# Band attention by pairs of heads in one pipeline over all tiles, its inputs made inside the last recurrence turns

## The chip, the cores and the metric

One core of one Trainium2 chip runs the whole program. The time is device microseconds of one execution; the kernel before has a median of 4641.96 us over 3 runs (4640.98 to 4644.14). Its engines are TensorE (PE, with its weight loads as PEld), VectorE (DVE), ScalarE (ACT), GpSimd (POOL) and SyncE (SP, which only issues transfers here).

## The reference

One layer of a streaming encoder, for a prompt of 2048 frames and a sample group of 32 frames. A combined projection feeds an RWKV-7 recurrence and a band attention; both are gated, merged and followed by an MLP. The change touches the attention (8 heads of 64):

```python
def band_attend(q, k, v, bias, valid):
    s = jnp.einsum("bqhd,bkhd->bhqk", q, k).astype(jnp.float32) * ATT_SCALE + bias
    s = jnp.where(valid, s, jnp.finfo(jnp.float32).min)
    p = jax.nn.softmax(s, axis=-1).astype(v.dtype)
    return jnp.einsum("bhqk,bkhd->bqhd", p, v)
```

In the prompt each chunk of 64 frames attends to its own chunk and the 8 before it. In the sample group 32 new frames attend to 256 cached frames and themselves. The bias comes from a table of relative distances, one row for each head.

## The kernel before

The program is a row of stages: modulation and first norm; the projection's first 14 row tiles; the recurrence in 34 turns of 64 frames (`build_rwkv`, line 1045), in which turns 1 to 28 also carry the projection's remaining 28 row tiles; the two final states (`store_states`, line 1178); the attention; the merge; the MLP. Stages are blocks, and a block begins when all engines have ended the one before. Inside a block each engine runs its own list in the order in which the code was written, and semaphores (`Steps`, line 65) tie the lists together.

A recurrence turn (`tensor_turn`, line 925) is a chain of small 64x64 products, each of which waits for VectorE or ScalarE to take the last result. `fill(n)` between the links issues up to n products of the projection. In turns 29 to 34 nothing is left to fill with, so `fill` does nothing there. On SP a turn loads the next rows (`sync_chunk`, line 674) and stores the output of the turn before it (`store_chunk`, line 679), which waits for VectorE's last step of that output.

The attention is `build_attention` (line 1211). `build_attention_inputs` (line 1227) loads q, k and v of all frames, turns v from channels to frames with TensorE transposes (L1285, copied out at L1303), turns the last 512 frames of k for an output (L1292), and makes the bias of each head by reversing rows of the table of distances (L1307). Then `build_attention_core` (line 1487) runs over 16 tiles of 128 queries, with up to 640 keys each: tiles 0 to 3 have 128, 256, 384 and 512 keys, tiles 4 to 15 have 640. For a tile VectorE copies the window of k and of v (L1522, L1529) and ScalarE the scaled queries (L1423).

Within a tile (class `Heads`, line 1340) the heads go one by one. TensorE makes the scores of a head from 64 rows of the array (L1460). VectorE adds the bias and takes the maximum (L1390). ScalarE takes the exponentials and their sum (L1433). VectorE makes the reciprocal (L1396) and scales the probabilities (L1399). TensorE turns them in five blocks (L1471), VectorE copies two blocks out (L1418) and ScalarE three (L1439). TensorE multiplies them with v (L1482): its stationary operand is the 128 columns of v of two heads, of which 64 output rows are used. The order on each engine is written out in `Heads.__init__`; head h's transposes are followed by the scores of head h+2 and by head h's values. At a tile's end ScalarE copies the result out (L1444) and stores it. A further block does the 32 sample queries against 288 keys in the same way, after loading and turning the cache (L1563 to L1584).

## Time and profile before

| what | us |
|---|---|
| median of 3 runs | 4641.96 |
| the profiled execution | 4652.85, of which the span is 4651.1 |
| start to the end of the projection's first part | 533.0 |
| recurrence turns 1 to 28 | 1312 |
| recurrence turns 29 to 34 and the states | 197.3 |
| attention (inputs, 16 tiles, sample tile) | 589.3 |
| merge and MLP | 2019.5 |

TensorE is busy for 91% of the span, DVE for 38%, ACT for 29%, POOL for 11%. [...]

### The profile page before, as it was taken

Reading aid. Unit: us, or ns where it says so; the run is one execution under the profiler, and the core shown is the slowest. Engines: PE = TensorE matmul, PEld = TensorE weight load, DVE = VectorE, ACT = ScalarE, POOL = GpSimd, SP = SyncE. Lnnn points to the kernel's source line nnn. Section 1 sums busy time; section 2 is a strip of 40 time slices with the busy share of each in tenths; the row PEclk is TensorE's granted clock in tenths of the full one; section 3 lists DMA queues with packets and bytes.
Section 4 is the critical chain, followed back from the end, with each engine's and each line's share of the span. In section 5 each row is a group of like instructions: output and inputs, shape, how many; then the busy total and the mean of one; then the engine's idle time right before and its main releaser. Section 6 shows DMA issues by size and latency. Waiting matters only on the chain. (4 is left out here: it accounts for less than half of the span.)

```text
span 4651.1 us, 83037 instructions
## 1 busy us (share of the span) xinstructions
PE 4222.8 (91%) x34634; PEld 3823.3 (82%) x34634; DVE 1763.5 (38%) x3403; ACT 1329.0 (29%) x2378; POOL 532.3 (11%) x518
## 2 busy tenths in 40 slices
PE   6799799999999999748888699979999999999998
PEld 2499688888888888746666489969999999999997
DVE  3500033333333333434555443335354453453542
ACT  2311122222222222103344321234343343443432
POOL 2211122332323232300000000000000000000000
PEclk9899899999999999665899699989999999999999
DMA  6522221212121211040000333334334344343342
GB/s 220 169 70 70 52 53 43 54 43 54 43 54 43 56 43 44 15 141 27 9 9 7 95 117 121 98 104 130 110 109 138 114 120 125 108 143 109 109 128 78
DMA packets 595783, 392.82 MB, mean 84 GB/s; under 512 B 99312, under 2 KB 585352, under 8 KB 594448
## 3 DMA queue, kind: packets, MB, share of 16 engines
q1 hardware_dynamic: 528336, 309.63, 23.6%
q10 hardware_dynamic: 67136, 78.63, 4.9%
q8 instruction: 246, 4.03, 0.4%
q14 instruction: 65, 0.53, 0.0%
HBM read 306.87 MB, written 81.34 MB: 83 GB/s over the span
## 5 line engine op out<-in xcount | busy, mean ns | idle before, releaser
L527 PE MATMUL proj_ps<-h_hi,w_hi 128*128 128x416 f32 x1680 | 619.8, 369 | 13.4 <-POOL w_lo L512 13.4
L527 PE MATMUL proj_ps<-h_lo,w_hi 128*128 128x416 f32 x1680 | 600.2, 357 | 0.0
L527 PE MATMUL proj_ps<-h_hi,w_lo 128*128 128x416 f32 x1680 | 596.2, 355 | 0.0
L1999 DVE TENSOR_TENSOR ff_lo<-ff_raw,ff_hi 128x1024 fp32r<-128x1024 f32 x320 | 391.5, 1224 | 450.1 <-ACT ff_hi L1995 449.8
L1600 PE MATMUL ff_ps<-h_hi,ff_hi 128*128 128x416 f32 x1280 | 462.8, 362 | 25.0 <-DVE ff_lo L1999 23.9
L1995 ACT ACTIVATE ff_hi<-ff_raw 128x1024 fp32r<-128x1024 f32 x320 | 337.7, 1056 | 454.4 <-PE ff_ps L1600 432.7
L1600 PE MATMUL ff_ps<-hidden_hi,ff_hi 128*128 128x416 f32 x1280 | 459.5, 359 | 3.8 <-DVE ff_lo L1999 3.8
L1600 PE MATMUL ff_ps<-h_hi,ff_lo 128*128 128x416 f32 x1280 | 452.4, 353 | 0.0
L1600 PE MATMUL ff_ps<-hidden_hi,ff_lo 128*128 128x416 f32 x1280 | 451.7, 353 | 0.0
L1600 PE MATMUL ff_ps<-h_lo,ff_hi 128*128 128x416 f32 x1280 | 448.3, 350 | 0.0
L1600 PE MATMUL ff_ps<-hidden_lo,ff_hi 128*128 128x416 f32 x1280 | 447.3, 349 | 0.0
L527 PEld LDWEIGHTS proj_ps<-h_hi,w_hi 128*128 128x128 f32 x1680 | 316.1, 188 | 32.2 <-issue 13.6
L527 PEld LDWEIGHTS proj_ps<-h_hi,w_lo 128*128 128x128 f32 x1680 | 316.4, 188 | 8.0
L527 PEld LDWEIGHTS proj_ps<-h_lo,w_hi 128*128 128x128 f32 x1680 | 317.6, 189 | 5.0
L935 PEld LDWEIGHTS wkv_ps<-solve 64*64 64x64 f32 x6336 | 213.7, 140 | 74.7 <-issue 53.8
L1600 PEld LDWEIGHTS ff_ps<-h_hi,ff_hi 128*128 128x128 f32 x1280 | 241.0, 188 | 36.4 <-DVE ff_lo L1999 21.7
L935 PE MATMUL wkv_ps<-solve 64*64 64x64 f32 x6336 | 245.8, 228 | 15.3 <-ACT solve L845 15.2
L1600 PEld LDWEIGHTS ff_ps<-hidden_hi,ff_hi 128*128 128x128 f32 x1280 | 240.3, 188 | 11.8 <-DVE ff_lo L1999 5.2
L1600 PEld LDWEIGHTS ff_ps<-h_lo,ff_hi 128*128 128x128 f32 x1280 | 241.5, 189 | 8.7 <-issue 5.1
L1600 PEld LDWEIGHTS ff_ps<-hidden_lo,ff_hi 128*128 128x128 f32 x1280 | 240.6, 188 | 8.8 <-issue 5.1
L1600 PEld LDWEIGHTS ff_ps<-h_hi,ff_lo 128*128 128x128 f32 x1280 | 240.6, 188 | 1.9
L1600 PEld LDWEIGHTS ff_ps<-hidden_hi,ff_lo 128*128 128x128 f32 x1280 | 240.0, 188 | 1.7
(285 smaller groups left out, 6587.8 us busy)
## 6 DMA issues: line engine op xcount, KB each, us to landing
ff_raw<-in_w_ff SPq DMA_DIRECT2D x320, 512.0 KB, 4.1
keep_proj<-proj_out ACTq DMA_DIRECT2D x210, 208.0 KB, 1.9
ada_w<-in_w_ada SPq DMA_DIRECT2D x24, 1024.0 KB, 5.7
w_raw<-in_w_in SPq DMA_DIRECT2D x42, 512.0 KB, 4.7
gates<-keep_proj SPq DMA_DIRECT2D x80, 208.0 KB, 2.5
rows_in<-keep_proj SPq DMA_DIRECT2D x32, 448.0 KB, 6.0
x_then_x<-keep_xT SPq DMA_DIRECT2D x40, 208.0 KB, 2.5
keep_x2T<-x_then_x ACTq DMA_DIRECT2D x40, 208.0 KB, 1.9
```

The lines of the kernel that those rows point to most:

```text
L527: mm = pe.matmul(self.ps[u][:, 0:BW], w[:, par, kk, :], a[:, kk, cols], start=(kk == 0 and j == 0), stop=(kk == KD - 1 and j == 2))
L935: mm = pe.matmul(self.bank[bank][rows, at + j * C:at + (j + 1) * C], lhs[rows, j, :], rhs[rows, j, :], start=True, stop=True)
L1600: mm = pe.matmul(out, w(i), x(kt), start=(first and i == 0 and j == 0), stop=(last and i == n - 1 and j == 2))
L1995: w.hi_s.done(act.activation(w.whi[:, s % 2], w.raw[:, s % 4], ACT.Copy), s)
L1999: w.lo_s.done(dve.tensor_tensor(w.wlo[:, s % 2], w.raw[:, s % 4], w.whi[:, s % 2].bitcast(F32), ALU.subtract), s)
```

## The change

Two things are changed.

First, the attention's inputs are made inside turns 29 to 33 by a new class `AttentionInputs`. The first recurrence block's setup also makes the table of distances, scaled by 8. q, k, v and the bias lie where the projection's inputs were, which are dead by then. In each of these turns there are five slots. In a slot TensorE makes four transposes of 128x128 in the place of the old filling work, and ScalarE copies the result out in the place where it used to take a projection result. There are 24 slots: 17 for v, 2 for the cache's k, 5 for the k output. VectorE reverses two heads' bias at the end of each of four turns. SP loads what the slots need between its own loads and stores.

Second, the core works on a pair of heads at once, and one software pipeline of 68 pairs plus two closing rounds runs over all 16 prompt tiles and the sample tile, with no block boundary and no loop between them. In round i TensorE makes the scores of pair i, the transposes of the first head of pair i-1, the values of pair i-2, and the transposes of the second head of pair i-1. Scores of the two heads use rows 0 to 63 and 64 to 127 of the array, by turns; values of the two heads use columns 0 to 63 and 64 to 127, by turns. q, k and v are read where they lie, so the three copies for a tile are gone. The probabilities are no longer scaled: the sums of a tile's 8 heads are inverted by one instruction, spread over 64 rows each by 8 products (L1512 after), copied by ScalarE, and multiplied into the result by VectorE, once for a tile.

The diff, cut to its core (the classes `Heads` and the functions `build_attention_inputs` and `build_attention_core` of before are removed, and `build_attention` is empty):

```diff
@@ build_rwkv
+    prep = AttentionInputs(outer, nc, k, pj, FILLED + RT + 1)
...
+                    if t > FILLED:
+                        prep.sync_turn(sp, t - FILLED - 1)
...
                             pj.evacuate(act, t + RT + 1, 1 - par, b)
+                        else:
+                            prep.scalar_slot(act, SLOTS * (t - FILLED - 1) + b)
...
+                    if t > FILLED:
+                        prep.vector_turn(dve, t - FILLED - 1)
...
-                    products = pj.products(pe, t + RT + 1, 1 - par) if filled(t) else iter(())
+                    products = pj.products(pe, t + RT + 1, 1 - par) if filled(t) else prep.products(pe, t - FILLED - 1)
...
+    build_attention_core(nc, k, prep)
...
+class AttentionInputs:
...
+    def sync_turn(self, sp, i):
+        if i == 0:
+            self.pj.mm_s.wait(sp, NB - 1, self.last)
+            self.pj.wait_stored(sp, IN_T)
+        for n in range(SLOTS * i, min(SLOTS * i + SLOTS, self.staged)):
+            kind, j = self.slots[n]
+            if n >= STAGES:
+                sp.wait_ge(self.turned, n - STAGES + 1)
...
+            sp.dma_start(out, src).then_inc(self.loaded[n % STAGES], 16)
+        if i < NH // 2:
+            for h in (2 * i, 2 * i + 1):
+                if h >= 2:
+                    sp.wait_ge(self.bias_turned, h - 1)
...
+            sp.dma_start(self.kT, self.rows[:, KT_:KT_ + NP, :]).then_inc(self.qk_loaded, 16)
+            sp.dma_start(self.qT, self.rows[:, QT:QT + NP, :]).then_inc(self.qk_loaded, 16)
...
+    def products(self, pe, i):
+        for n in range(SLOTS * i, SLOTS * i + SLOTS):
+            for place in range(3 * KD):
+                if place == KD and n < len(self.slots):
+                    self.tensor_slot(pe, n)
+                yield
...
+            mm = pe.transpose(ps[0:src.shape[1], a * P:(a + 1) * P], src, self.k.ident[:, :])
+        mm.then_inc(self.turned, 1)
...
+            act.activation(self.V[0:rows_of_tile(j), j, :], ps[0:rows_of_tile(j), :], ACT.Copy).then_inc(self.kept, 1)
...
+                dve.tensor_copy(self.bias[:, h, :], self.rev[:, h % 2, ::-1]).then_inc(self.bias_turned, 1)
...
+def build_attention_core(nc, k, a):
...
+                def scores(i):
+                    b, j = pair(i)
+                    if i >= 1:
+                        biased.wait(pe, 1, i - 1)
+                    halves = [b.keys(rows, j) for rows in HALVES]
+                    for n in range(len(halves[0])):
+                        for h, rows in enumerate(HALVES):
+                            x0, x1, keys = halves[h][n]
+                            mm = pe.matmul(ps_s[h][0:b.nq, x0:x1], a.qT[rows, j, b.cols], keys, start=True, stop=True)
+                    made_scores.done(mm, "s")
+
+                def turned(i, h):
+                    b, j = pair(i)
+                    exped.wait(pe, h, i)
+                    if i + h >= 1:
+                        front_kept.wait(pe, 1 - h, i - 1 + h)
+                        back_kept.wait(pe, 1 - h, i - 1 + h)
+                    for c, n in b.chunks:
+                        part = c // (2 * P) if c < 2 * P else 1
+                        at = c - 2 * P * part
+                        mm = pe.transpose(ps_t[0:n, part, at:at + b.nq], e[0:b.nq, i % 2, h, c:c + n], k.ident[0:b.nq, 0:b.nq])
+                    made_turned.done(mm, h)
+
+                def values(i):
+                    b, j = pair(i)
+                    front_kept.wait(pe, 1, i)
+                    back_kept.wait(pe, 1, i)
+                    if j == 0 and b.t >= 1:
+                        normed.wait(pe, "y", b.t - 1)
+                    if j == 0 and b.sample:
+                        pe.wait_ge(sample_loaded, 32)
+                    for n, (c, size) in enumerate(b.chunks):
+                        for h, rows in enumerate(HALVES):
+                            mm = pe.matmul(ps_y[rows, j, 0:b.nq], b.values(c, size, slice((2 * j + h) * HD, (2 * j + h + 1) * HD)),
+                                           eT[0:size, i % 2, h, c:c + b.nq], start=(n == 0), stop=(n == len(b.chunks) - 1))
+                    made_values.done(mm, "y")
+                    if j == NP - 1:
+                        divided.wait(pe, "r", b.t)
+                        for jj in range(NP):
+                            for h, rows in enumerate(HALVES):
+                                mm = pe.matmul(ps_r[rows, jj, 0:b.nq], rec[0:b.nq, b.t % 2, 2 * jj + h:2 * jj + h + 1].broadcast_to([b.nq, HD]),
+                                               k.ident[0:b.nq, 0:b.nq], start=True, stop=True)
+                        spread.done(mm, "r")
+
+                for i in range(N + 2):
+                    if i < N:
+                        scores(i)
+                    if 1 <= i <= N:
+                        turned(i - 1, 0)
+                    if i >= 2:
+                        values(i - 2)
+                    if 1 <= i <= N:
+                        turned(i - 1, 1)
...
+                def add_bias(i, h):
+                    b, j = pair(i)
+                    made_scores.wait(dve, "s", i)
+                    if i >= 2:
+                        made_turned.wait(dve, h, i - 2)
+                    dve.memset(idle[:, 0, 2 * (i % 2) + h:2 * (i % 2) + h + 1], 0.0)
+                    biased.done(dve.tensor_tensor_reduce(e[0:b.nq, i % 2, h, b.c0:b.c1], ps_s[h][0:b.nq, b.c0:b.c1], bias(b, 2 * j + h),
+                                                         -(HD ** -0.5), 3.0e38, ALU.add, ALU.min,
+                                                         nmax[0:b.nq, b.t % 2, 2 * j + h:2 * j + h + 1]), h)
+
+                def keep_front(i, h):
+                    b, j = pair(i)
+                    made_turned.wait(dve, h, i)
+                    if i >= 2:
+                        made_values.wait(dve, "y", i - 2)
+                    ins = take_turned(dve.tensor_copy, b, i % 2, h, 0)
+                    front_kept.done(dve.memset(idle[:, 1, 2 * (i % 2) + h:2 * (i % 2) + h + 1], 0.0) if ins is None else ins, h)
+
+                def divide(t):
+                    exped.wait(dve, 1, t * NP + NP - 1)
+                    nq = bands[t].nq
+                    divided.done(dve.reciprocal(rec[0:nq, t % 2, :], total[0:nq, t % 2, :]), "r")
+
+                def norm(t):
+                    spread_kept.wait(dve, "r", t)
+                    if t >= 2:
+                        dve.wait_ge(stored[t % 2], 16 * (t // 2))
+                    nq = bands[t].nq
+                    normed.done(dve.tensor_tensor(yT[:, t % 2, :, 0:nq], ps_y[:, :, 0:nq], rb[:, :, 0:nq], ALU.mult), "y")
+
+                for i in range(N + 2):
+                    if i < N:
+                        add_bias(i, 0)
+                    if 1 <= i <= N:
+                        keep_front(i - 1, 0)
+                    if i < N:
+                        add_bias(i, 1)
+                    if 1 <= i <= N:
+                        keep_front(i - 1, 1)
+                        if i % NP == 0:
+                            divide(i // NP - 1)
+                    if i >= 2 and (i - 2) % NP == NP - 1:
+                        norm((i - 2) // NP)
...
+                def exponentials(i, h):
+                    b, j = pair(i)
+                    biased.wait(act, h, i)
+                    s = e[0:b.nq, i % 2, h, b.c0:b.c1]
+                    at = 2 * j + h
+                    exped.done(act.activation(s, s, ACT.Exp, bias=nmax[0:b.nq, b.t % 2, at:at + 1], scale=-1.0,
+                                              accum_out=total[0:b.nq, b.t % 2, at:at + 1]), h)
...
+                def keep_spread(t):
+                    spread.wait(act, "r", t)
+                    if t >= 1:
+                        normed.wait(act, "y", t - 1)
+                    nq = bands[t].nq
+                    spread_kept.done(act.activation(rb[:, :, 0:nq], ps_r[:, :, 0:nq], ACT.Copy), "r")
+
+                for i in range(N + 2):
+                    if 1 <= i <= N:
+                        keep_back(i - 1, 0)
+                    if i < N:
+                        exponentials(i, 0)
+                        exponentials(i, 1)
+                    if 1 <= i <= N:
+                        keep_back(i - 1, 1)
+                    if i >= 2 and (i - 2) % NP == NP - 1:
+                        keep_spread((i - 2) // NP)
```

The order of TensorE inside a full tile. The names are the scores' banks, the turned probabilities' bank and the output's bank; "x5" means five such instructions in a row. Before, one head in the loop over tiles, transposes of head h, scores of head h+2, values of head h:

```order
L1471 MATMUL probs_ps<-identity,probs 128x128 x5
L84 REGISTER_ALU
L1460 MATMUL scores_ps<-k_window,q_tile 128x512
L1460 MATMUL scores_ps<-k_window,q_tile 128x128
L84 REGISTER_ALU
L84 ISA
L84 REGISTER_ALU x2
L1482 MATMUL att_ps<-probs_turned,v_window 128x128 x5
```

After, the last round of a tile, with its closing products:

```order
L1480 MATMUL scores_ps<-kT,qT 128x512 x2
L1480 MATMUL scores_ps<-kT,qT 128x128 x2
L1492 MATMUL probs_ps<-identity,scores 128x128 x5
L1505 MATMUL proj_ps<-probs_turned,v_rows 64x128 x10
L1512 MATMUL proj_ps<-identity,prob_recips 64x128 x8
L1492 MATMUL probs_ps<-identity,scores 128x128 x5
```

One head's group was 5 transposes, 2 scores and 5 values. Now a round holds 4 scores, 5 transposes, 10 values and 5 transposes for two heads, and one round in four also the 8 products that spread the reciprocals. The rows L84, which move registers and waits for the loop over tiles, are gone.

The order of SP from turn 28 to turn 30, with the semaphores that each transfer waits for. `keep_yrT` is the store of a turn's output, `rows_in` the load of a later turn's rows. Before:

```order
L681 DMA keep_yrT<-yr_out 128x4x64 [waits state_dve]
L676 DMA rows_in<-keep_proj 128x14x64 [waits front_pool]
L681 DMA keep_yrT<-yr_out 128x4x64 [waits state_dve]
L676 DMA rows_in<-keep_proj 128x14x64 [waits front_pool]
L681 DMA keep_yrT<-yr_out 128x4x64 [waits state_dve]
```

After:

```order
L682 DMA keep_yrT<-yr_out 128x4x64 [waits state_dve]
L677 DMA rows_in<-keep_proj 128x14x64 [waits front_pool]
L1304 DMA att_rows_in<-keep_proj 128x4x128 [waits proj_stored1,proj_stored0,proj_mm]
L1304 DMA att_rows_in<-keep_proj 128x4x128 x4
L1309 DMA bias_backwards<-keep_ext 128x640 x2
L1312 DMA kT<-keep_proj 128x4x2080
L1313 DMA qT<-keep_proj 128x4x2080
L682 DMA keep_yrT<-yr_out 128x4x64 [waits state_dve]
L677 DMA rows_in<-keep_proj 128x14x64 [waits front_pool]
L1304 DMA att_rows_in<-keep_proj 128x4x128
```

The first loads for the slots wait for the projection's last store. They, the bias rows and the two large loads of k and q now stand between the rows of turn 30 and the output store of turn 28. In turn 30 the slots' loads follow the row load, which follows that store.

## Rows read from the trace of the kernel before

**Rows 1.** Windows: us, busy PE, PEld, DVE, ACT, POOL (instructions), PEclk, DMA, GB/s.
```profile
2042.30:2107.60 65.30, 20.81 (x92) 14.81 (x92) 18.24 (x32) 3.60 (x6) 0.00 (x0) 0.55 0.82 275
2107.60:2208.00 100.40, 86.62 (x350) 66.26 (x352) 43.15 (x199) 38.40 (x107) 0.00 (x0) 0.59 0.03 9
2146.70:2179.40 32.70, 29.18 (x106) 23.32 (x106) 11.56 (x51) 11.22 (x28) 0.00 (x0) 0.50 0.03 9
2208.00:2590.70 382.70, 327.05 (x1824) 248.31 (x1822) 211.97 (x599) 152.50 (x324) 0.00 (x0) 0.89 0.03 8
2590.70:2631.60 40.90, 24.54 (x96) 16.19 (x96) 10.80 (x52) 8.41 (x29) 0.00 (x0) 0.54 0.12 34
```

**Rows 2.** Timeline, one head of a full tile: start us, us, engine, line, operation.
```profile
2351.09 1.34 PE L1460 MATMUL scores_ps<-k_window,q_tile 64*128 64x512 f32 x4
...
2352.36 1.38 PE L1482 MATMUL att_ps<-probs_turned,v_window 128*128 128x128 f32 x10
2352.47 0.82 DVE L1390 CUSTOM_DVE_ANT_0 scores<-scores_ps,bias 128x640 f32<-128x640 f32 x1 [0.20 <-issue]
...
2353.34 0.83 ACT L1433 ACTIVATE probs<-scores,minus_max 128x640 f32<-128x640 f32 x1 [1.65 <-DVE minus_max L1390]
...
2353.58 0.71 PE L1471 MATMUL probs_ps<-identity,probs 128*128 128x128 f32 x5
...
2354.22 1.34 PE L1460 MATMUL scores_ps<-k_window,q_tile 64*128 64x512 f32 x4
2354.32 0.49 ACT L1439 ACTIVATE probs_turned<-probs_ps 128x384 f32<-128x384 f32 x1
2354.32 0.42 DVE L1418 COPY probs_turned<-probs_ps 128x256 f32<-128x256 f32 x1 [1.02 <-PE probs_ps L1471]
```

**Rows 3.** Waits of PE in the twelve full tiles: total us, times, longest.
```profile
PE probs_ps L1471 <- ACT probs L1433: 34.8, 11, 3.2
```

**Rows 4.** Timeline of TensorE in a late turn, products over 64 rows.
```profile
1992.97 0.42 PE L956 MATMUL wkv_ps<-lora_w_in,w_a_up 64*128 64x64 f32 x1
...
1993.18 0.42 PE L956 MATMUL wkv_ps<-lora_w_in,w_a_up 64*128 64x64 f32 x1
1993.19 0.42 PE L957 MATMUL wkv_ps<-rows_mixed,w_a_up 64*128 64x64 f32 x1
```

**Rows 5.** Windows of 10 us where the granted clock rises.
```profile
2180.00:2190.00 10.00, 7.51 (x29) 5.38 (x26) 4.34 (x16) 3.55 (x9) 0.00 (x0) 0.50 0.08 26
2190.00:2200.00 10.00, 10.00 (x60) 7.75 (x61) 6.16 (x24) 3.90 (x10) 0.00 (x0) 0.96 0.01 2
```

**Rows 6.** Timeline and DMA issues: the attention's inputs.
```profile
2047.54 1.97 PE L1285 MATMUL v_ps<-identity,vT 128*128 128x128 f32 x8 [0.17 <-DMA vT<-keep_proj]
...
qT<-keep_proj SPq DMA_DIRECT2D x1, 4160.0 KB, 29.4
```

**Rows 7.** Late turns: first and last start, last projection store, output store, row loads.
```profile
L956 PE MATMUL wkv_ps<-lora_w_in,w_a_up x32: 417/418/473, 1881.9 to 1994.0; 64*128 64x64 f32 x32
...
1846.33 0.34 ACTq L541 DMA_DIRECT2D keep_proj<-proj_out  x1
...
1988.55 0.38 SPq L681 DMA_DIRECT2D keep_yrT<-yr_out  x1
...
rows_in<-keep_proj SPq DMA_DIRECT2D x3, 448.0 KB, 4.3
```

**Rows 8.** Softmax passes of tiles 0 to 3, min/median/max ns.
```profile
L1433 ACT ACTIVATE probs<-scores,minus_max x32: 385/554/723, 2108.0 to 2202.6; 128x128 f32<-128x128 f32 x8, 128x256 f32<-128x256 f32 x8, 128x384 f32<-128x384 f32 x8, 128x512 f32<-128x512 f32 x8
```

**Rows 9.** Timeline of the sample tile: loads, scores, last store.
```profile
2595.44 0.46 SPq L1564 DMA_DIRECT2D v_window<-in_cache_att_v  x1
2600.07 1.57 PEld L1572 LDWEIGHTS scores_ps<-identity,cache_k_rows 128*128 128x128 f32 x8 [9.62 <-DMA v_window<-in_cache_att_v]
...
2603.56 1.17 PE L1460 MATMUL scores_ps<-k_window,q_tile 64*32 64x288 f32 x4 [1.51 <-DVE k_window L1581]
...
2629.42 0.39 ACTq L1446 DMA_DIRECT2D keep_yaT<-att_turned  x1
```

More of the change, by code:

```diff
@@ new lines, with __init__, keys, values @@
+class Band:
+    def __init__(self, a, t):
+        self.t, self.sample = t, t == NQ
+        self.nq = DEC if self.sample else P
+        self.c0, self.c1 = (0, SKEYS) if self.sample else (max(KT5 - 1 - t, 0) * P, BAND)
+        self.cols = slice(t * P, t * P + self.nq)
+        self.chunks = [(c, min(P, self.c1 - c)) for c in range(self.c0, self.c1, P)]
+        self.a = a
+    def keys(self, rows, j):
+        a = self.a
+        if self.sample:
+            return [(0, PAST, a.Kc[rows, j, :]), (PAST, SKEYS, a.kT[rows, j, SEQ:NT])]
+        at = (self.t - KT5 + 1) * P
+        return [(x0, x1, a.kT[rows, j, at + x0:at + x1]) for x0, x1 in ((self.c0, 512), (512, BAND)) if x1 > x0]
+    def values(self, c, n, cols):
+        a = self.a
+        if self.sample:
+            return a.Vc[:, c // P, cols] if c < PAST else a.V[0:n, NQ, cols]
+        return a.V[0:n, self.t - KT5 + 1 + c // P, cols]
@@ new lines, in build_attention_core @@
+        spread = Steps(ctx, nc, "att_recips_spread", ["r"])
+        biased = Steps(ctx, nc, "att_biased", [0, 1])
+        exped = Steps(ctx, nc, "att_exped", [0, 1])
+        front_kept, back_kept = Steps(ctx, nc, "att_turned_front_kept", [0, 1]), Steps(ctx, nc, "att_turned_back_kept", [0, 1])
+        divided = Steps(ctx, nc, "att_sums_divided", ["r"])
+        spread_kept = Steps(ctx, nc, "att_recips_kept", ["r"])
+        normed = Steps(ctx, nc, "att_normed", ["y"])
+        bands = [Band(a, t) for t in range(TILES)]
@@ new lines, in pair, with bias, take_turned @@
+        def pair(i):
+            return bands[i // NP], i % NP
+        def bias(b, h):
+            return sbias[:, h, :] if b.sample else a.bias[:, h, b.c0:b.c1]
+        def take_turned(copy, b, par, h, part):
+            first, full, last = b.c0 // P, b.c1 // P, (b.c1 + P - 1) // P
+            ins = None
+            for n, t0, t1 in ((P, first, full), (b.c1 - full * P, full, last)):
+                t0, t1 = max(t0, 2 * part), min(t1, (2, KT5)[part])
+                if t1 > t0:
+                    out = eT[0:n, par, h, t0 * P:t1 * P].rearrange("p (c t) -> p c t", t=P)[:, :, 0:b.nq]
+                    ins = copy(out, ps_t[0:n, part, (t0 - 2 * part) * P:(t1 - 2 * part) * P].rearrange("p (c t) -> p c t", t=P)[:, :, 0:b.nq])
+            return ins
@@ L1278, in _ @@
+                sp.dma_start(a.Vc, k.cache_v.rearrange("(c p) h d -> p c (h d)", p=P)).then_inc(sample_loaded, 16)
+                out = k.yaT.rearrange("(a p) t -> p a t", p=P)
+                for t, b in enumerate(bands):
+                    normed.wait(sp, "y", t)
+                    sp.dma_start(out[:, :, b.cols], yT[:, t % 2, :, 0:b.nq]).then_inc(stored[t % 2], 16)
+                for j in range(2):
+                    sp.wait_ge(stored[j], 16 * ((TILES + 1 - j) // 2))
             @block.tensor
@@ L1300, in _ @@
-                dve.tensor_copy(ext[:, near:EXT], tab[:, 2 * REL:2 * REL + 1].broadcast_to([NH, EXT - near])).then_inc(made, 1)
-                for j in range(NQ + 1):
-                    dve.wait_ge(turned, j + 1)
-                    dve.tensor_copy(a.V[0:size(j), j, :], pv[j % 2][0:size(j), :]).then_inc(kept, 1)
-                    if j % 2 == 1:
-                        h = j // 2
-                        dve.wait_ge(back[h % 4], 16 * (h // 4 + 1))
-                        dve.tensor_copy(a.bias[:, h, :], rev[:, h % 4, ::-1]).then_inc(bias_turned, 1)
@@ L1595, in split_products, with build_attention @@
+def build_attention(nc, k):
+    pass
 def split_products(pe, out, hi, lo, x_hi, x_lo, kts, first=True, last=True):
```

457 lines of the change are left out of this document (147 added, 310 removed).

## The prediction

> **What bounds the kernel now.** I read the page's row of the granted clock first, then windows cut at the stages, then the timeline inside one tile, then the waits of TensorE. The windows [rows 1] split the stage that changes: 65.3 us until the first bias is added, in which TensorE is busy for 20.8; 100.4 us for tiles 0 to 3 at a mean granted clock of 0.59; 382.7 us for the twelve full tiles at 0.89, 31.9 us each; 40.9 us for the sample tile.
>
> Inside a full tile at full clock TensorE is the bound [rows 2]: the scores of a head start at 2351.09, its neighbour's values at 2352.36, the next transposes at 2353.58, the next scores at 2354.22. So scores hold TensorE for 1.27 us, values 1.22, five transposes 0.64, together 3.13 us a head or 25.0 us for eight. [...]
>
> Every stage is a block, so what shortens the attention moves merge and MLP forward unchanged; nothing there is touched. The whole saving shows in the time.
>
> **The start (removed: 65.3 us; added: about 7).** The input block goes. What is left before the first bias is the sample's two loads and one VectorE copy, which waits for both. The same kind of pair takes 4.6 us from the second issue to use in the sample tile [rows 9], plus 0.5 for the first issue; the copy moves the same 32x2304 elements as now, which I put at 1.3 us. That is 6.4 us in place of 65.3: -58.9. The table of distances moves to the recurrence's setup, a chain of two transfers in a block that has a load and a transpose of its own; I take +1 us.
>
> **Turns 29 to 33 (added).** A turn lasts 37 us, a third of 1881.9 to 1992.5 over three turns [rows 7]. Five slots of four transposes come in. [...] Slots 3 to 5 stand where TensorE waits for a copy anyway; the first stands ahead of the link RH, and nothing hides it. ScalarE's copies of 512 columns stand in the chain as the evacuations did. I charge half, 2 us a turn, and 1 us a turn for the first slot's load: it is issued behind the output store (1988.55), the row load and its own issue, lands some 5 us later as row loads do (4.3) [rows 7], and TensorE asks at about 1994.2. That is 15 us for five turns. Once, in turn 29, the wait is longer: the first load waits for the projection's last store, issued at 1846.33 [rows 7]; store (2.3) and load (3) put its landing at about 1852, and TensorE asks at 1846.6. Queued behind that waiting slot is the whole turn: +5. k and q take 29.4 us to land [rows 6], from about 1853 to 1882, just before turn 30's rows and slots are wanted; behind them I see no stall. The eight reversals on VectorE fall between the turn's last VectorE step and the next turn's first product and cost nothing. If that cover went they would cost 4. Sum +20. Bounds: 0 (all hidden, or paid back by a warmer clock) and 45 (24 slots at 0.9 and a copy of 0.6 in the chain, 5 and 5 for loads).
>
> **A full tile (the largest term).** Scores of the two heads lie in rows 0 to 63 and 64 to 127. The trace has such a pair already: L956 and L957 start 0.01 us apart, and the next pair follows after 0.21 us [rows 4]. So two heads' scores should hold TensorE as long as one head's do now, 1.27 us. For values the stationary operand is halved to 64 columns and the two heads sit side by side. No row shows two products that share all 128 rows and differ in columns alone; the nearest are the scores' halves above and the 64x64 quarters of the recurrence, which use both. Bounds: 1.22 us for both heads if they overlap, 2.44 if not; I take 1.22. Transposes stay 0.64 for each head. A pair then holds TensorE for 1.27 + 1.22 + 2 x 0.64 = 3.77 us, against 6.26 now.
>
> Do the waits allow this? I lay one round out from the durations of rows 2: scores to bias 1.39 (their duration and 0.05), bias with its memset and read 0.87, exponentials with the read 0.95, VectorE's copy 0.42, ScalarE's 0.49. With scores at 0: bias of head 0 to 2.26, transposes of the older pair from 1.27 to 1.98, VectorE's copy to 2.70, bias of head 1 to 3.57, next scores possible from 3.62. ScalarE: copy to 2.50, exponentials to 3.45, second exponentials 3.61 to 4.55, copy to 5.04, which is 1.25 into the next round, where TensorE asks for it at 1.27. So both chains close just inside TensorE's 3.77, and the round is 3.8 us. Four rounds are 15.2. A tile's close adds eight pairs of products of 128 columns, 1.0 us, and its ScalarE copy and VectorE multiplication delay the next bias by about half a microsecond, of which 0.4 reaches TensorE: 16.6 us a tile at full clock. The copies of k, v and q (3.0 us of VectorE) and the scaling (0.55 a head) are gone from the path.
>
> [...] Which share of the time is slow? Now it is about 0.2 (0.89 granted). The long seam of 3.2 us is gone, but TensorE no longer has slack against the other engines, and short gaps may come in each round. I take a quarter: 0.75 / 16.6 + 0.25 / 30 tiles a microsecond, 18.7 us a tile, 224 us for twelve against 382.7: -158.7. Bounds: 199 and 360.
>
> **Tiles 0 to 3.** [...] In tile 0 ScalarE is longer, since an exponential pass of 128 keys takes 0.39 us [rows 8] and its read 0.19: 2.3. The clock starts low, as now. It rose in tile 3, when TensorE had no gap for some microseconds (busy 7.51 of 10 us at 0.50, then 10.00 at 0.96) [rows 5]; tile 2, at 29.2 of 32.7 us busy, stayed at 0.50 [rows 1]. I take tiles 0 and 1 slow and 2 and 3 half way to 3.0 and 3.4: 4 x (2.3 + 3.2 + 3.7 + 4.5) + 7 of closes = 62 against 100.4: -38.4. Bounds 51 and 71.
>
> **Sample tile.** No block edge, no cache loading in front. A round is scores 1.17 [rows 9] and two biases with a copy between, 2.6 us; four are 10.4, and the last pair's way out (exponentials, transposes, values, spread, copy, multiplication, store of 2.2 from 2629.42 to the block's end [rows 1, 9]) 6.8. 17.2 against 40.9: -23.7, give or take 5.
>
> **Sum.** -58.9 + 1 + 20 - 158.7 - 38.4 - 23.7 = -258.7. The profiled execution took 4652.85 us (span 4651.1 and 1.75 around it), 10.9 above the median. 4652.85 - 258.7 = 4394; less 10.9, 4383 us beside the median.
>
> **Rivals.**
> [...]
> [...]
> *The values' halves don't overlap.* A round is 1.22 longer at full clock and 2.2 at half: 21.5 and 39 a tile, 24.2 at the same mix; +66 and +10 in the short tiles: 4459 us. Nothing in the trace excludes it.
> *The round is bound by the semaphores, not by TensorE.* The three engines hand over six times a round and my layout closes within 0.1 us. If a round is 4.6 us, TensorE has gaps of 0.8 in each and I put the slow share at 0.4: 0.6 / 19.8 + 0.4 / 30, 22.9 a tile: +50, 4433 us.
> *Slower.* Neither halves overlap, and the low clock holds. Then a round is 4.3 + 4.3 + 2.1 + 0.4 = 11.1 us, a tile 47, against 31.9 now; full tiles +340 and short ones +39 on the forecast: 4762 us. It decides once a full tile takes over 37 us. The rows of L956 and L957 speak against half of it.
>
> **How the numbers follow.** Forecast 0.57, low clock 0.18, values one after the other 0.10, semaphores 0.11, slower 0.03, about no change 0.01. The range reaches down to 4330, where tiles run at full clock (199 and 51) and the turns grow by little, and up to 4530, the low-clock case. A measurement of this kernel can tell 0.2%, about 9 us, from no change. All cases but one lie over 100 us below 4642: faster 0.96, same 0.01, slower 0.03.
>
> **What would show it.** In the profile after: no input block, first bias about 7 us into the attention block; turns 29 to 33 at 39 to 42 us with TensorE waiting about 5 us once for `att_rows_in`; products of the two heads starting within 0.02 us of each other, in L1480 and in L1505; a round of 3.8 us where the clock is 1.00; full tiles at 18.7 us with a granted clock near 0.88; about 17 us for the sample. It is wrong if the clock in the full tiles is near 0.5, if L1505's instructions come one after another, or if turns 29 to 33 grow by more than 45 us.

## The result and the profile after

The changed kernel takes 4326.45 us, median of four runs (4325.18 to 4331.74), against 4643.05 us for the kernel before (4640.98 to 4648.82). The ratio is 0.9315, 95% interval 0.9303 to 0.9326: faster, by 317 us. I had forecast 4383 us with a range from 4330 to 4530. The direction was right, and so was what was to make a tile shorter; the time is 57 us below the forecast and just below the range.

The profiled execution took 4331.74 us (span 4329.7). First the windows of the kernel after, cut as [rows 1] cut the one before (the start, tiles 0 to 3, the full tiles, the sample tile), then three windows of 10 us in tiles 0 and 1. Columns as in [rows 1].

```profile
2043.28:2049.56 6.28, 0.80 (x4) 0.53 (x4) 1.35 (x1) 0.00 (x0) 0.00 (x0) 0.50 0.52 130
2049.56:2095.48 45.92, 43.00 (x365) 29.66 (x366) 20.53 (x133) 30.35 (x97) 0.00 (x0) 0.84 0.06 19
2095.48:2292.48 197.00, 196.94 (x2006) 144.56 (x2006) 120.86 (x408) 132.31 (x300) 0.00 (x0) 1.00 0.06 18
2292.48:2310.64 18.16, 13.20 (x178) 10.61 (x178) 6.83 (x38) 7.43 (x28) 0.00 (x0) 0.79 0.08 20
...
2050.00:2060.00 10.00, 9.41 (x48) 5.69 (x48) 3.38 (x35) 6.01 (x28) 0.00 (x0) 0.50 0.00 0
2060.00:2070.00 10.00, 9.19 (x80) 6.27 (x78) 3.79 (x27) 5.60 (x19) 0.00 (x0) 0.80 0.09 29
2070.00:2080.00 10.00, 9.25 (x99) 6.93 (x99) 5.21 (x32) 7.50 (x21) 0.00 (x0) 1.00 0.10 29
```

The third row is the one to look at: in 197.00 us of full tiles TensorE is busy for 196.94 and the granted clock is 1.00, full speed. Before it was busy for 327.05 of 382.7 at 0.89. The clock is a share of full speed; the records of all these kernels hold 0.50 and 1.00 and nothing else, and a mean between them is a mix of the two. The last three rows show where the full clock begins: the mean of 0.80 in the second of them is 4 us at 0.50 and 6 at 1.00, so it begins some 14 us after the first bias, in tile 1. The kernel before was at 0.50 until tile 3 [rows 5], 83 us after its first bias.

The terms, forecast and measured, in us (profiled executions):

| part | before | after | difference | forecast |
|---|---|---|---|---|
| turns and setup (to the core's first load) | | | +1.0 | +21 |
| start, to the first bias | 65.3 | 6.3 | -59.0 | -58.9 |
| tiles 0 to 3 | 100.4 | 45.9 | -54.5 | -38.4 |
| twelve full tiles | 382.7 | 197.0 | -185.7 | -158.7 |
| sample tile | 40.9 | 18.2 | -22.7 | -23.7 |
| merge and MLP | 2019.5 | 2019.1 | -0.4 | 0 |
| span | 4651.1 | 4329.7 | -321.4 | -258.7 |

The timeline of TensorE over one round and a tile's close, the counterpart of [rows 2] (start us, us, engine, line, operation; each product stands as two instructions, here as before, so x8 are the four score products of two heads):

```profile
2179.97 1.35 PE L1480 MATMUL scores_ps<-kT,qT 64*128 64x512 f32 x8
2181.25 0.77 PE L1492 MATMUL probs_ps<-identity,scores 128*128 128x128 f32 x5
2181.94 1.31 PE L1505 MATMUL proj_ps<-probs_turned,v_rows 128*64 128x128 f32 x20
2183.09 1.04 PE L1512 MATMUL proj_ps<-identity,prob_recips 128*64 128x128 f32 x16
2184.06 0.76 PE L1492 MATMUL probs_ps<-identity,scores 128*128 128x128 f32 x5
2184.76 1.35 PE L1480 MATMUL scores_ps<-kT,qT 64*128 64x512 f32 x8
2186.04 0.76 PE L1492 MATMUL probs_ps<-identity,scores 128*128 128x128 f32 x5
2186.73 1.31 PE L1505 MATMUL proj_ps<-probs_turned,v_rows 128*64 128x128 f32 x20
2187.97 0.77 PE L1492 MATMUL probs_ps<-identity,scores 128*128 128x128 f32 x5
2188.67 0.70 PE L1480 MATMUL scores_ps<-kT,qT 64*128 64x512 f32 x2
```

No row has a bracket with idle time: each group starts as the one before it ends. Both heads' scores hold TensorE for 1.28 us (2179.97 to 2181.25), as long as one head's did [rows 2]; both heads' values for 1.24 us (2186.73 to 2187.97) with 20 instructions where one head's 10 took 1.22. A round from scores to scores is 3.91 us (2184.76 to 2188.67), the round with the close 4.79. The transposes of a head hold TensorE for 0.69 to 0.70 us, before for 0.64 [rows 2]. VectorE's normalisations (L1560) come every 16.53 us from tile 3 to tile 14.

The start, and the one new wait that I had named, in the timeline of the kernel after:

```profile
2043.28 0.35 SPq L1461 DMA_DIRECT2D sample_bias_backwards<-keep_ext  x1
...
2043.68 0.45 SPq L1462 DMA_DIRECT2D cache_v<-in_cache_att_v  x1
2048.17 1.35 DVE L1529 COPY sample_bias<-sample_bias_backwards 32x2304 f32<-32x2304 f32 x1 [7.95 <-DMA cache_v<-in_cache_att_v]
```
```profile
1853.38 1.09 PE L1346 MATMUL proj_ps<-identity,att_rows_in 128*128 128x128 f32 x4 [4.71 <-DMA att_rows_in<-keep_proj]
```

The copy waits for the two loads (2048.17, 4.5 us after the second issue) and the first bias follows it at 2049.56. TensorE waits 4.71 us for the first rows in turn 29, near the 5 that I put down, and twice more for such rows in later turns, 2.58 and 2.12 us.

### The profile page after: what moved, and what is told of

Its sections match the earlier page's. It is cut to its first block and busy times, and to the rows that moved or that the text cites. A ratio compares the mean times of both kernels' runs of the same rounds, so it can differ in the third digit from the quotient of the medians.

```text
span 4329.7 us, 82396 instructions
## 1 busy us (share of the span) xinstructions
PE 4013.8 (93%) x34922; PEld 3657.2 (84%) x34922; DVE 1634.0 (38%) x3112; ACT 1307.2 (30%) x2363; POOL 532.4 (12%) x518
```

## The experiments

All are edits of the changed kernel. Medians are of all runs of a kernel, to be read against the 4326.45 of the changed kernel and the 4327.04 of its repetition; "tile" is the mean time between VectorE's normalisations of tiles 3 to 14. A median is that of four or five executions, of which one was profiled. Two stretches of unchanged code differ between the profiled executions: the last turns by some 5 us (below), and the stretch from the last normalisation to the end, 2021.6 us in the changed kernel and 2017.0 in its repetition, from 2012.8 to 2022.5 over all the kernels of the table. So a difference of a few microseconds between two medians says nothing by itself.

| kernel | median us | tile us | clock in full tiles | ratio to before, 95% |
|---|---|---|---|---|
| changed kernel | 4326.45 | 16.53 | 1.00 | 0.9303 to 0.9326 |
| the same again | 4327.04 | 16.53 | 1.00 | 0.9313 to 0.9339 |
| inputs apart | 4391.93 | 16.53 | 1.00 | 0.9449 to 0.9481 |
| drained | 4403.91 | 20.84 | 0.99 | 0.9461 to 0.9500 |
| long gap | 4418.79 | 22.22 | 0.88 | 0.9504 to 0.9545 |
| short gap | 4349.17 | 17.65 | 1.00 | 0.9358 to 0.9386 |
| values in sequence | 4370.42 | 19.35 | 1.00 | 0.9402 to 0.9434 |
| scores in sequence | 4333.67 | 16.55 | 1.00 | 0.9313 to 0.9348 |
| transposes doubled | 4389.17 | 20.90 | 1.00 | 0.9439 to 0.9473 |
| slots doubled | 4332.23 | 16.53 | 1.00 | 0.9319 to 0.9350 |
| bias copy late | 4325.81 | 16.53 | 1.00 | 0.9314 to 0.9339 |
| cached keys first | 4324.95 | 16.53 | 1.00 | 0.9309 to 0.9334 |
| both of these | 4325.35 | 16.53 | 1.00 | 0.9301 to 0.9334 |

### Is the clock kept up by the missing gap?

The first theory (G) is that before's low stretches came from the gap at each seam; its rival (M) is that the denser mix of instructions holds the clock by itself. In the trace of the kernel before, the first gap of the full tiles and the windows of the low stretches at it and at the next gap (which ends at 2247.09):

```profile
2212.32 1.32 PE L1471 MATMUL probs_ps<-identity,probs 128*128 128x128 f32 x5 [3.16 <-ACT probs L1433]
...
2211.40:2224.90 13.50, 12.58 (x42) 9.40 (x43) 4.41 (x14) 3.54 (x8) 0.00 (x0) 0.50 0.00 0
...
2249.00:2252.20 3.20, 3.20 (x16) 3.02 (x15) 0.83 (x3) 0.92 (x2) 0.00 (x0) 0.50 0.00 0
```

All twelve falls of the clock in the full tiles begin in the gap at a seam (3.2 us in eleven of them, 2.8 in the last) or within about 2 us of its end. That goes with G and doesn't prove it. So the pipeline was drained at each tile, in all three engines' loops:

```diff
-                for i in range(N + 2):
-                    if i < N:
+                for t, r in ((t, r) for t in range(TILES) for r in range(NP + 2)):
+                    i = NP * t + r
+                    if r < NP:
                         scores(i)
```

> The pipeline of rounds is emptied at the end of each tile and filled again, so a seam returns in which TensorE waits; every instruction stays. Both theories price a full tile at 22 to 23 us where the clock stays full (16.5 now, two extra part rounds of about 3 us). Theory G (the low clock of before's tiles came from the gap at the seams, so the seamless order is what holds it at 1.00): granted clock of the full tiles falls to 0.8 to 0.9 and a tile takes 25 us or more, total about +105 to +130 us. Theory M (the denser mix of pairs holds the clock at 1.00 whatever the gaps): clock 1.00, 22.5 us a tile, total about +85 to +95 us with the short tiles and the sample.

Windows over tiles 5 to 15 of the drained kernel (from the normalisation of tile 4 to that of tile 15), one window in it, and its waits there (total us, times, longest):

```profile
2144.00:2374.70 230.70, 187.76 (x1856) 135.26 (x1852) 113.13 (x374) 120.52 (x276) 0.00 (x0) 0.99 0.04 14
```
```profile
2164.00:2174.00 10.00, 7.64 (x43) 4.43 (x43) 5.36 (x17) 4.84 (x11) 0.00 (x0) 0.83 0.09 27
```
```profile
PE scores_ps L1480 <- DVE minus_max L1539: 18.6, 11, 1.7
PE probs_ps L1492 <- ACT probs_turned L1593: 14.3, 19, 0.8
PE proj_ps L1505 <- ACT probs_turned L1593: 7.4, 11, 0.7
```

TensorE is idle for a fifth of the time, in gaps of up to 1.7 us, and the clock is still 0.99; it falls for some 3 us in only two of the eleven tiles (0.83 over 10 us), which take 22.1 and 22.2 in place of 20.7 us. The mean of 20.84 us is less than the 22 to 23 that both theories gave. That looks like M. But the gaps here are half as long as before's. So the next kernel has the seamless order and one gap of before's length in each tile; VectorE's writes of zeros are extra work and go nowhere.

```diff
+                        if i >= 6 and i % NP == 2:
+                            pe.wait_ge(seam, GAP * ((i - 2) // NP))
...
                         norm((i - 2) // NP)
+                        if i < N:
+                            for g in range(GAP):
+                                if i > 5 or g:
+                                    dve.wait_ge(seam, GAP * ((i - 5) // NP) + g)
+                                dve.memset(pause[:, :], 0.0).then_inc(seam, 1)
```

> In the changed kernel, once in every tile, TensorE waits at the pair after a tile's normalisation until VectorE has written five rows of 512 zeros into a scrap tile (0.5 us each): one gap of about 3 us a tile, the length of the gaps at the old seams (3.2), and nothing else is different. Theory G (a gap of this length takes the clock down, and the seamless order is what kept it up): each tile shows a stretch at 0.5, granted clock of the full tiles 0.85 to 0.93, a tile 16.5 + 3 + 2 to 4 for the slow stretch, 21.5 to 23.5 us, total +75 to +110 us. Theory M (the mix holds the clock whatever the gap; in the drained kernel gaps of up to 1.7 us and TensorE busy 81% left it at 0.99): clock 1.00, tiles 19.3 to 19.7 us, total about +45 us.

The timeline at one gap, the waits over tiles 5 to 14, and windows over the same stretch and right behind the gap:

```profile
2194.48 1.33 PE L1494 MATMUL probs_ps<-identity,scores 128*128 128x128 f32 x5 [3.65 <-DVE pause L1584]
```
```profile
PE probs_ps L1494 <- DVE pause L1584: 36.5, 10, 3.6
```
```profile
2145.70:2368.30 222.60, 186.13 (x1686) 137.70 (x1682) 126.17 (x390) 109.47 (x250) 0.00 (x0) 0.88 0.04 13
```
```profile
2194.50:2198.50 4.00, 4.00 (x27) 3.34 (x28) 1.86 (x6) 2.13 (x5) 0.00 (x0) 0.50 0.00 0
```

Behind the gap the five transposes take 1.33 us in place of 0.76, and the clock is 0.50 for these 4 us; then it comes back. The same 1686 instructions hold TensorE for 186.13 us, against 165.24 in the changed kernel, where the clock is 1.00. A tile costs 16.53 + 3.65 + 2.0 us, the last term being the clock. Then the same with one write in place of five (GAP = 1):

> As the kernel with the gap at each tile, but VectorE writes one row of 512 zeros in place of five: TensorE waits 0.5 to 1.5 us once a tile (3.65 us there, granted clock 0.88, tiles alternating between 21.7 and 22.7 us). Theory G, as the drained kernel and that one bear it out (the length of the longest gap decides, 1.7 us is mostly held, 3.2 and over is not): clock 1.00 in all full tiles, a tile 16.5 + 0.5 to 1.5, total +8 to +20 us. Rival (any regular gap takes the clock down): granted clock below 0.95, a tile over 19 us, total over +40 us.

```profile
PE probs_ps L1494 <- DVE pause L1584: 10.5, 10, 1.0
```
```profile
2129.13:2305.60 176.47, 166.01 (x1686) 121.46 (x1682) 106.77 (x350) 108.34 (x250) 0.00 (x0) 1.00 0.06 16
```

A gap of 1.0 us in each tile costs 1.1 us and leaves the clock alone (the median rose by 22.7 us, a little over the 20 that I gave). So G holds for the long gap and not for any gap: the clock fell behind TensorE's gaps of 3.2 us (before) and 3.65 us (here), seldom with gaps of up to 1.7 us (twice in eleven tiles), never with 1.0. What follows a gap may matter too: before, a low stretch lasted 3.4 or 13.7 us (once 6.8), here by turns 3.4 and 6.8. Which of the differences between the two kernels does that was not tested.

### Do transposes hold the clock down?

They hold TensorE for 0.35 of a round (2 x 0.69 of 3.91 us), before for 0.20 of a head's 3.13 us (0.64, [rows 2]). So they were all made twice:

```diff
-                    for c, n in b.chunks:
+                    for c, n in b.chunks * 2:
```

> The core's transposes of the probabilities are all made twice (into the same place), so they hold about half of TensorE's time in place of a third. [...] Forecast's theory (only gaps and the low level before them matter; TensorE stays without a gap): clock 1.00, a round 3.92 + 10 x 0.13 = 5.3 us, a tile 22 us, total about +75 to +85 us.

```profile
2131.88:2340.88 209.00, 209.00 (x2085) 165.09 (x2082) 104.47 (x341) 109.94 (x250) 0.00 (x0) 1.00 0.05 14
```

With 2.5 of 5.0 us of each round in transposes, the clock is 1.00 without a break. A tile takes 20.90 us, somewhat less than the 22 that I gave. So fp32 transposes that alternate with other products don't hold the clock down here. A long stretch of transposes alone was not run.

### Do the halves of the array work side by side?

The two loops over chunks and heads are exchanged, once for the values and once for the scores:

```diff
-                    for n, (c, size) in enumerate(b.chunks):
-                        for h, rows in enumerate(HALVES):
+                    for h, rows in enumerate(HALVES):
+                        for n, (c, size) in enumerate(b.chunks):
```

> The products with the values run head after head (10 chunks' products in column half 0, then in column half 1 of the array) in place of alternating. Theory O (products of the two column halves run at the same time, which is why L1505's twenty... ten products a pair hold TensorE for 1.3 us): the group takes 2.4 to 2.6 us, a round is 1.2 us longer, a full tile about 21.4 us, total about +65 to +75 us. Theory S (the size of a product, not its neighbour, sets the 1.3 us): no change, within 5 us of 4326.

The timeline of TensorE with the values in sequence:

```profile
2224.97 2.02 PE L1505 MATMUL proj_ps<-probs_turned,v_rows 128*64 128x128 f32 x20
2226.92 0.77 PE L1492 MATMUL probs_ps<-identity,scores 128*128 128x128 f32 x5
2227.61 1.35 PE L1480 MATMUL scores_ps<-kT,qT 64*128 64x512 f32 x8
```

The same 20 instructions take 2.02 us in place of 1.31 and a tile 2.83 us more: products in the two column halves do run side by side when they alternate, and the median rose by 44 us. I had expected 2.4 to 2.6 us, no overlap at all, and so too much. The starts in the trace show what is left of the overlap. Alternating, the two halves' products start 0.007 us apart and the next two 0.109 us later. In sequence one row of ten starts, 0.109 us apart, runs from 2224.97 to 2226.00 and a second row of ten from 2225.68 to 2226.71: the second half began while three instructions of the first had still to start, and overlapped with these alone.

> The score products run head after head (both key pieces in array rows 0 to 63, then both in 64 to 127) in place of alternating; everything else as in the changed kernel. Theory O (neighbours in the two row halves run at the same time): from the run with the values in sequence, where a group went from 1.31 to 2.02 us, I expect the scores to go from 1.35 to 1.9 to 2.6 us, a round 0.5 to 1.2 us longer, total +30 to +75 us. Theory S (the order makes no difference): within 5 us.

The scores didn't change: 1.36 against 1.35 us a group, 16.55 against 16.53 a tile. The median is 7 us higher; the profiled execution is 2.6 us longer in its span, and its turns are 2.8 us longer (below), so the core has no part in that. For the rest of the 7 us there is no trace. The edit did change the program's order. With only two products a head the second head's still overlap the first's: both heads together take what one took before [rows 2]. The trace agrees with the starts above: the second head's first product starts 0.013 us behind the first head's, with that head's other three instructions still to come. So the order matters for ten instructions a head in sequence and not for four; theory O was right about the overlap and wrong about the order.

### What do the slots cost the turns?

The slots, loads and reversals moved into a block of their own behind the states:

```diff
-                    products = pj.products(pe, t + RT + 1, 1 - par) if filled(t) else prep.products(pe, t - FILLED - 1)
+                    products = pj.products(pe, t + RT + 1, 1 - par) if filled(t) else iter(())
...
+            for i in range(SLOTS):
+                for _place in prep.products(pe, i):
+                    pass
```

> The slots, loads and reversals of the inputs leave turns 29 to 33 and stand in a block of their own behind the states; the attention core is the new one, untouched. Forecast's theory (the slots cost the turns 20 us net): the turns and their setup end about 20 us sooner than in the changed kernel. Rival W (the slots warm TensorE's clock, and what they add comes back in quicker products): the turns keep their 198 us within 5 us and their granted clock falls from 0.82 back to about 0.71. Either way the new block costs 45 to 65 us and the core keeps its length (267.7 us from its start to the merge, full tiles at 16.5 us). Total by W about +55 us on the changed kernel's 4326, by the forecast's theory about +35.

and, the other way, each slot's transposes made twice:

```diff
-        for a in range(NP):
+        for a in list(range(NP)) * 2:
```

> Each slot's four transposes are made twice (into the same place, so the result is the same): 24 x 4 more transposes in turns 29 to 33. Theory W (slots warm the clock and are paid back): turns grow by under 6 us, granted clock there rises from 0.82 to 0.88 or more. Theory H (slots are hidden only where TensorE waits anyway, the clock has no part): the clock stays near 0.82, and the growth is 24 slots at 0.6 to 0.9 us less what is hidden, 10 to 20 us. The core is unchanged.

The block apart lasts 59.0 us (2041.53 to 2100.55). The profiled execution's span is 53.8 us longer than the changed kernel's, near the 55 of theory W, and the median rose by 65. Granted clock in 1850 to 2030 us, for inputs apart, the changed kernel and slots doubled:

```profile
1850.00:2030.00 180.00, 135.88 (x2594) 123.79 (x2594) 77.11 (x194) 35.36 (x86) 49.90 (x56) 0.73 0.06 12
```
```profile
1850.00:2030.00 180.00, 140.39 (x2738) 124.17 (x2738) 81.89 (x203) 47.57 (x111) 49.60 (x55) 0.84 0.36 113
```
```profile
1850.00:2030.00 180.00, 143.47 (x2756) 127.92 (x2756) 80.00 (x197) 47.53 (x110) 49.67 (x55) 0.87 0.35 113
```

The slots go with a warmer clock: more work, yet few more busy microseconds. The turns are the same code in nine of the kernels, and their length (first product of turn 29 to the core's first load) follows the clock that each run happened to be granted in that stretch:

| kernel | turns, us | clock 1850 to 2030 |
|---|---|---|
| before | 196.7 | 0.72 |
| inputs apart (no slots) | 195.2 | 0.73 |
| changed, and transposes doubled | 195.7, 195.7 | 0.84, 0.83 |
| changed again; values, scores in sequence | 197.9, 198.4, 198.5 | 0.80, 0.80, 0.79 |
| long gap, bias copy late, drained, short gap | 199.9, 200.3, 200.5, 201.0 | 0.77, 0.76, 0.76, 0.76 |
| slots doubled | 200.4 | 0.87 |
| cached keys first; both | 190.6; 196.4 | 0.85; 0.78 |

Within the nine, 0.08 of clock is worth 5.3 us. Carried on to 0.73 (an estimate from these rows), turns with slots would take about 203 us against 195.2 without: 7 to 8 us for the 24 slots and their waits at an equal clock. The doubled slots say the same from the other end: 200.4 us where the line gives about 194 at 0.87, 7 us for 24 slots more. What the nine take is 198.7 on average, 2 to 3.5 us more than the two kernels without slots, since the warmer clock gives back the rest. Theory W is right in kind. Whether the clock gives everything back is open: by the traces 2 to 3.5 us are left, but they are one execution of each kernel without slots, and by the medians the kernel without slots is 65 - 59, about 6 us, slower outside its new block. Both differences lie within what unchanged code varies by.

### Two small changes that might go further

The sample's bias copy moved from ahead of the first bias to round NP + 2; the cached keys in the first slots (two, not the four of my expectation), whose loads need not wait for the projection's stores:

```diff
+                    if i == NP + 2:
+                        dve.wait_ge(sample_loaded, 32)
+                        dve.tensor_copy(sbias[:, :, :], a.srev[:, :, ::-1]).then_inc(sbias_ready, 1)
```
```diff
-        self.slots = [("v", j) for j in range(NQ + 1)] + [("c", c) for c in range(PAST // P)] + ...
+        self.slots = [("c", c) for c in range(PAST // P)] + [("v", j) for j in range(NQ + 1)] + ...
```

> Two small changes meant to be faster: the sample's bias copy, which now waits for two loads before the first bias of tile 0, moves to the third round of tile 1; and the cached keys take the first four slots in turn 29, so that TensorE's first slot doesn't wait for a load queued behind the projection's last store. First: first bias 4 to 5 us earlier (2.2 us into the block in place of 6.3). Second: of TensorE's 4.7 us waits for the row load in turn 29 one goes, 0 to 4 us. Together 4 to 9 us below the changed kernel (4317 to 4322 us) if both are on the path; the turns vary by 2 us from run to run, so the profile has to show each. Rival: the start is bound by the fetch of the block's code on each engine, and only 1 to 2 us are won.

> Only the sample's bias copy moves behind the second tile's start (the combined version had this and the cached keys first, and its core was 4.7 us shorter in the profile with no difference in its median). Theory C (the copy's wait is on the path): first bias 1 us into the block in place of 6.3, from the block's start to the last full tile's normalisation 4 to 5 us less, total -4 to -5 us. Rival (the start's gain is given back by a colder clock in tile 0): core within 2 us of the changed kernel.

> Only the order of the slots changes: the four of the cached keys stand first in turn 29, so that the first rows loaded don't have to wait for the projection's last store. Theory D (TensorE's wait for the row load, 4.7 us in turn 29, is on the path): it falls below 2 us and turns 29 to 33 take 3 to 5 us less, total -3 to -5 us. Rival (the turns are bound by hops of the clock, 2 us up or down from run to run): no change within 3 us.

> The changed kernel once more, unaltered, on the same chip as the two below, to compare them by. 4326 us, within 5 us; turns 29 to 33 and their setup within 2.5 us of 196 from the first product of turn 29 to the attention block, tiles as before.

Late copy: the first bias comes 0.9 us into the block, and from the block's start to tile 15's normalisation it is 251.8 us against 256.0: 4.2 us won in the profile. Cached keys first: TensorE's waits for row loads, 9.4 us in the changed kernel with 4.7 the longest, become two kinds:

```profile
PE proj_ps L1347 <- DMA att_rows_in<-keep_proj: 5.4, 2, 2.8
PE proj_ps L1347 <- DMA att_rows_in<-in_cache_att_k: 1.8, 1, 1.8
```

and the turns lie 4 us (190.6 at 0.85) and 3 us (196.4 at 0.78) under the line of the nine. None of the three medians is distinguishable from the changed kernel's: the turns alone differ by 5 us between runs of equal code, more than either change, and the merge and MLP by up to 10. The profiles say that both stand on the path; the times don't show a version that beats the changed kernel.

## Why the prediction was right, and where it was wrong

*The start, the sample.* Right within 1 us each, by the rows that were named for them.

*A tile at full clock.* 16.6 us forecast, 16.53 measured, and that it is so near is in part luck: the round is 3.91 in place of 3.8, which makes +0.44 in four, and the close takes 0.88 in place of 1.4. The close holds TensorE for about the time of its products; the 0.4 us more for a delayed bias didn't come. The round is longer by its two groups of transposes, 0.69 to 0.70 us each in place of 0.64. A group's first start comes 0.20 us behind the last start of the group before it, against 0.11 within a group, and the second start is late too (0.165 behind the first). Before, the transposes followed values of the same 128x128 shape, and had neither: 0.11 and 0.109. That scores of two heads take the time of one [rows 4], that values do the same by column halves, and that both chains close inside TensorE's round, all hold. The values at 1.22 us were my choice between bounds of 1.22 and 2.44, with no row behind it; values in sequence show what the worse bound would have begun to cost.

*The share of slow time: the step that failed, 27 us of the 63.* I wrote that TensorE "no longer has slack against the other engines, and short gaps may come in each round", and took a quarter. In the full tiles TensorE is idle for 0.06 of 197.00 us and the slow share is nil. The short-gap kernel adds that short gaps would not have mattered: 1.0 us in every tile leaves the clock at 1.00. Rows 3 had the answer: before's falls come with the long gap at the seam, which the change removes, and my own 16.6 for a tile rested on there being no gap. The low bound of 199 us for the twelve tiles was the outcome (197.0). No run shows the 30 us that the sum, and with it the prices of the rivals, takes for a tile at the low clock: no full tile of any run lies wholly at 0.50. What the runs show is 3.4 to 13.7 us at 0.50 at a time, in which five transposes take 1.32 or 1.33 us, against 0.71 before and 0.76 after at 1.00.

*Tiles 0 to 3, 16 us.* The same step: I kept tiles 0 and 1 slow and 2 and 3 half. TensorE is busy for 9.41 of the first 10 us, and the clock is at 1.00 some 14 us after the first bias. In before's tile 2, at 29.2 of 32.7 us, it was 0.50 [rows 1]. No run shows the sum's rounds of 3.2, 3.7 and 4.5 us for tiles 1 to 3; from scores to scores the trace has 2.0 to 2.2 us in tile 0 (2050.13 to 2056.50, at 0.50), where the sum has 2.3, and 2.6 for the first round of tile 1 (to 2059.09, still at 0.50).

*Turns 29 to 33, 20 us.* +20 was charged and +1 for the setup; the profiled executions differ by 1.0 together, the nine runs by 2 to 3.5 on average. The waits for rows came about as charged: 4.71 us for the 5 in turn 29, 2.58 and 2.12 for the 5 of the other turns. The sum's 2 us a turn stand for about half of five slots of 0.9 us: by the trace a slot's four transposes take 1.09 us at 0.50 (1853.38) and 0.66 at 1.00 (1859.41). What failed is the rest of the sum: by the estimate above all of it together, waits included, costs 7 to 8 us at an equal clock in place of 20, so the waits for rows and the slots' transposes and copies lie for the most part in time in which the turn waits anyway. The clock, 0.76 to 0.84 in place of 0.72, gives back most of what is left. My lower bound had the warmer clock in it; I gave it no weight.

The three misses, 27 + 16 + 20, make up the difference of 63 us between -258.7 and -321.4, and all three lean on the same side. In the first two, and in the smaller part of the third, I took the clock as it was granted before (0.89 in the full tiles, 0.59 in tiles 0 to 3 [rows 1], 0.72 in the turns) for a property of the stage; the larger part of the third, about 12 us, is work that was hidden. Of the rivals none came: the clock didn't stay low, the column halves overlap, the round is not bound by semaphores (TensorE has no wait in the full tiles), and nothing took over 37 us.

## What to carry to other kernels

When a change takes away the gap behind which the profile shows the clock falling, price the new stage at the full clock (here 1.00 came in place of 0.89), and keep the old share of slow time only for gaps that stay; ask of each gap how long it is, since on this kernel 1.0 us cost only itself and 3.65 us cost another 2.0. Independent work laid into a latency-bound chain cost less than its busy time here: by the estimate above 7 to 8 us at an equal clock for 24 slots, whose transposes alone take 0.66 us a slot at 1.00; and the clock with it was 0.76 to 0.84, against 0.72 and 0.73 without. Take such work out and double it to see its price. Where equal code differs by 5 or 10 us between runs, read the granted clock of that stretch before giving a difference of the medians to an edit.

## What the hardware showed that I had not expected

- Products in the two column halves (128 rows, 64 columns) overlap fully when they alternate (20 instructions in 1.31 us) and partly when ten of one half precede ten of the other (2.02 us); the second half then starts three instructions ahead of the first half's end. Before, the 10 instructions of one head took 1.38 us.
- Score products in the two row halves overlap in either order when there are four instructions a head (1.35 and 1.36 us).
- Between groups whose products have different shapes (64x128, 128x128, 128x64) the next group's first start comes 0.20 us behind, in both kernels. Between groups of one shape it is 0.11 us (values to transposes before) or 0.10 (values to the close's products after), as within a group. A round has four such changes, 0.09 us each.
- With half of TensorE's time in transposes (2.5 of 5.0 us a round) the granted clock is 1.00 for 209 us.
- With TensorE busy for 81% of the time, in gaps of up to 1.7 us, the granted clock is 0.99; with one gap of 3.65 us a tile and 84% busy, 0.88. The length of the gap goes with the clock here, the share of busy time doesn't.
